# A 64-expert MoE on one core: the second expert product on column groups, and a sixteen-step pattern of heavy and light steps

## The chip, the core and the metric

The program runs on one core of a Trainium2 chip. The time is device microseconds of one execution; the kernel before took 1189.84 us (median of three runs, 1188.8 to 1190.72).

## What is computed

One layer of a hybrid decoder for 512 prompt tokens and 8 sample tokens (520 in all) of width 1024, in float32: a recurrent and convolutional mixer, cross-attention into 256 memory rows, and a mixture of experts, each followed by a residual and a layer norm. The change touches only the last:

```
scores = sigmoid(x @ w_router)                 # 64 experts, top 8 of each token, gates sum to 2.5
for each token t and each of its 8 experts e:
    h = silu(x[t] @ w1_e[e]) * (x[t] @ w3_e[e])        # 1024 -> 256, twice
    y[t] += gate[t, e] * (h @ w2_e[e])                 # 256 -> 1024
y += swiglu(x, w1_s, w3_s, w2_s)               # one shared expert
x = layer_norm(ALPHA * x + y)
```

520 tokens with 8 experts each make 4160 rows, 65 per expert on the mean. The weights of an expert are three matrices of 1 MB.

## The kernel before

Up to about 505 us the kernel does the mixer, the attention, the router and a sort of the experts by their number of rows. Then 64 steps follow, one per expert, and after them the sum over each token's eight rows and the last layer norm.

**Steps.** A step has one of three sizes. `LCAP` = 64 row slots is a light step, `MCAP` = 96 a heavy one, and `CAP` = 112 a big one, which is a heavy place among the first eight steps. The pattern has `NB` = 8 places with `LIGHT` = (2, 5, 7), so 24 experts get light steps and 40 heavy or big ones (35 heavy, 5 big). The sort gives the experts with the most rows to the heavy places. Should an expert have more rows than its step has slots, a second pass over all experts runs at the end (`n_max > CAP`; `bump` adds to the count what a step has less than 112).

**One step of TensorE** is written out as `step(e)`: `t_step(e-1)` transposes the hidden rows of the expert before; `c_step(e)` is the first product (`up_few`, `up_most` or `up`); `b_step(e+1)` transposes the gathered rows of the next expert; `y_step(e-1)` is the second product (`down_few` or `down`); `a_step(e+3)` finds the rows of the expert after (`find`, five small matmuls). `up_few` and `down_few` put two products of 64 columns side by side on the array's two column halves; `up_most` does so for 64 of its 96 slots, and puts the other 32 (`MORE`) four abreast on groups of 32 columns. The heavy second product is `down(..., MCAP)`: four matmuls of 96 columns by 512, on the whole array.

**The other engines.** ScalarE (ACT) copies the transposed rows (`xc`, `xc_part`), applies silu, copies the turned hidden rows (`hc_most`), and writes the left half of the result scaled by the gate (`yh`, L1650). VectorE (DVE) multiplies the hidden rows (`hd_most`, L2198), writes the right half of the result (`yh`, L2201), then turns found rows into indices (`indices`) and builds the one-hot rows of step e+5 (`oh`). GpSimd (POOL) waits for both halves of the result (`s_step`), scatters 64 rows and, of a heavy expert, the rest by `more_y` (L705), and only then issues the gather of expert e+3 (`g_step`, L692): 64 rows by `idx_x` and, for a heavy one, 32 more by `more_x`. TensorE's `b_step` waits for both.

**Weights.** SyncE (SP) has four weight slots. It issues the three loads of expert e+4 (L522 to L524) when the second product of expert e is done (`m_y`).

**The end.** When the scatter of expert 61 has landed, SP begins to load the 16 MB of `y_rows` back; TensorE sums them.

## Time and profile before

| | |
|---|---|
| median of 3 runs | 1189.84 us |
| profiled execution | 1188.33 us, of which the span from first to last instruction 1186.6 us |
| PE busy | 1129.1 us (95%) |
| DVE, ACT, POOL busy | 427.9, 256.9, 254.0 us |
| granted PE clock | 0.987 on the mean |
| HBM read and written | 300.15 and 29.36 MB |

Busy time says how long an engine had work, not what ended the program; for that the waits and the chain that ended last are read, and in the steps the order of work of TensorE beside the landing of what it needs. A PE record of a float32 matmul stands twice, since each is run as two passes.

### The profile page before, as it was taken

Reading aid. Unit: us, or ns where it says so; the run is one execution under the profiler, and the core shown is the slowest. Engines: PE = TensorE matmul, PEld = TensorE weight load, DVE = VectorE, ACT = ScalarE, POOL = GpSimd, SP = SyncE. Lnnn points to the kernel's source line nnn. Section 1 sums busy time; section 2 is a strip of 40 time slices with the busy share of each in tenths; the row PEclk is TensorE's granted clock in tenths of the full one; section 3 lists DMA queues with packets and bytes.
Section 4 is the critical chain, followed back from the end, with each engine's and each line's share of the span. In section 5 each row is a group of like instructions: output and inputs, shape, how many; then the busy total and the mean of one; then the engine's idle time right before and its main releaser. Section 6 shows DMA issues by size and latency. Waiting matters only on the chain.

```text
span 1186.6 us, 21423 instructions
## 1 busy us (share of the span) xinstructions
PE 1129.1 (95%) x8348; PEld 752.3 (63%) x8348; DVE 427.9 (36%) x1127; ACT 256.9 (22%) x533; POOL 254.0 (21%) x292
## 2 busy tenths in 40 slices
PE   7999996999999988989999999999999999999996
PEld 6888654877875767857765555555555565555521
DVE  0359998233039434661112222122222222221034
ACT  1101144013042124201122222222222222222210
POOL 3120050000000000032333333433323333333300
PEclk9999998999998999999999999999999999999999
DMA  9630304015045652185999999999999999999696
GB/s 331 250 142 1 152 21 177 1 75 227 1 143 176 250 214 108 73 286 197 365 408 392 396 383 394 402 399 388 383 386 402 393 384 384 381 401 387 260 369 279
DMA packets 67593, 319.16 MB, mean 269 GB/s; under 512 B 11591, under 2 KB 17951, under 8 KB 40909
## 3 DMA queue, kind: packets, MB, share of 16 engines
q1 hardware_dynamic: 51269, 278.60, 60.3%
q0 software_dynamic: 14848, 35.48, 7.9%
q10 hardware_dynamic: 1424, 4.35, 0.9%
q8 instruction: 37, 0.61, 0.2%
q14 instruction: 15, 0.12, 0.0%
HBM read 300.15 MB, written 29.36 MB: 278 GB/s over the span
## 4 chain that ended last, share of the span: by engine, by line
PE 74%; DVE 16%; DMA 4%; ACT 2%; SPq 2%; issue 1%; POOL 0%; DVEq 0%; POOLq 0%
PE psum L797 66%; PE psum L812 8%; DVE act_mem L1782 7%; DVE mk_mem L1944 2%; DMA arena<-y_rows 2%; DMA arena<-in_w_in_dram 1%; SPq L572 1%; DMA act_mem<-x_rows,more_x 1%; DVE act_mem L2000 0%; ACT act_mem L1565 0%; DVE act_mem L2151 0%; DVE act_mem L1879 0%; ACT act_mem L1574 0%; DVE act_mem L1796 0%; DVE act_mem L2163 0%
## 5 line engine op out<-in xcount | busy, mean ns | idle before, releaser
L797 PE MATMUL psum<-arena,act_mem 128*32 128x128 f32 (+6 forms) x4800 | 507.8, 361 | 0.9 <-ACT act_mem L1665 0.9
L797 PEld LDWEIGHTS psum<-arena,act_mem 128*32 128x32 f32 (+5 forms) x4800 | 259.7, 123 | 188.8 <-issue 107.9
L797 PE MATMUL psum<-act_mem,arena 128*128 128x260 f32 (+1 forms) x1728 | 355.1, 367 | 8.2 <-DMA arena<-in_w_in_dram 2.8
L797 PEld LDWEIGHTS psum<-act_mem,arena 128*128 128x128 f32 x1728 | 307.9, 194 | 52.8 <-DMA arena<-in_w_in_dram 3.0
L705 POOL DMA_INDIRECT y_rows<-act_mem,idx_y x39 | 45.9, 1177 | 239.3 <-DVE act_mem L2201 226.3
L812 PE MATMUL psum<-ident,act_mem 128*128 128x128 f32 (+6 forms) x484 | 80.0, 297 | 17.2 <-DVE act_mem L1883 6.8
L2201 DVE TENSOR_SCALAR act_mem<-psum,act_mem 96x512 f32<-96x512 f32 (+1 forms) x40 | 29.9, 747 | 159.7 <-PE psum L797 159.7
L1782 DVE SCALAR_TENSOR_TENSOR act_mem<-act_mem,wcb 128x511 f32<-128x511 f32 (+29 forms) x120 | 77.8, 729 | 0.0
L812 PEld LDWEIGHTS psum<-ident,act_mem 128*128 128x128 f32 (+6 forms) x484 | 58.5, 172 | 29.6 <-issue 13.7
L2198 DVE TENSOR_TENSOR act_mem<-act_mem,psum 128x192 f32<-128x192 f32 x35 | 12.4, 355 | 161.2 <-ACT act_mem L1636 161.2
L797 PEld LDWEIGHTS psum<-act_mem 128*96 128x96 bf16 (+7 forms) x419 | 31.3, 125 | 60.7 <-issue 59.7
L797 PE MATMUL psum<-act_mem 128*96 (+10 forms) x419 | 52.9, 264 | 0.8 <-DVE act_mem L2163 0.7
L1632 ACT ACTIVATE act_mem<-psum 128x768 f32<-128x768 f32 (+1 forms) x59 | 42.7, 724 | 45.6 <-PE psum L812 45.6
L1650 ACT ACTIVATE act_mem<-psum,act_mem 96x512 f32<-96x512 f32 (+1 forms) x40 | 27.4, 684 | 112.4 <-PE psum L797 112.4
L698 POOL DMA_INDIRECT y_rows<-act_mem,idx_y x23 | 25.3, 1102 | 117.0 <-DVE idx_x L2179 103.9
L1636 ACT ACTIVATE act_mem<-psum 128x192 f32<-128x192 f32 x35 | 11.6, 331 | 178.6 <-PE psum L797 178.6
L812 PE MATMUL psum<-ident,mk_mem 128*128 128x128 f32 (+5 forms) x316 | 43.6, 280 | 3.6 <-DVE mk_mem L1944 1.9
L812 PEld LDWEIGHTS psum<-ident,mk_mem 128*128 128x128 f32 (+5 forms) x316 | 36.9, 183 | 14.8 <-issue 12.4
L797 PE MATMUL psum<-arena,kv_mem 128*128 128x512 f32 x96 | 41.8, 593 | 1.2 <-ACT kv_mem L1454 1.2
L631 POOL MEMSET act_mem<- 128x512 f32 x1 | 0.5, 526 | 190.5 <-PE psum L812 190.5
L705 POOL DMA_INDIRECT y_rows<-act_mem,more_y x39 | 35.0, 897 | 11.9 <-issue 11.9
L692 POOL DMA_INDIRECT act_mem<-x_rows,idx_x x32 | 31.1, 973 | 15.0 <-issue 9.5
(282 smaller groups left out, 789.6 us busy)
## 6 DMA issues: line engine op xcount, KB each, us to landing
arena<-in_w_e_dram SPq DMA_DIRECT2D x192, 1024.0 KB, 9.8
arena<-y_rows SPq DMA_DIRECT2D x8, 2048.0 KB, 24.2
arena<-in_w_in_dram SPq DMA_DIRECT2D x16, 512.0 KB, 18.0
arena<-in_cache_mem_k_dram SPq DMA_DIRECT2D x8, 1024.0 KB, 8.6
arena<-in_cache_mem_v_dram SPq DMA_DIRECT2D x8, 1024.0 KB, 12.1
arena<-in_w_v_dram SPq DMA_DIRECT2D x1, 4096.0 KB, 24.7
arena<-in_w_k_dram SPq DMA_DIRECT2D x1, 4096.0 KB, 14.0
arena<-in_w_out_dram SPq DMA_DIRECT2D x1, 4096.0 KB, 14.0
```

The costliest lines, as they stand in the source:

```text
L572: sp.dma_start(y_in[t % 3][:, s], y.rearrange("(l s p) n -> s p l n", l=4, s=2)[s]).then_inc(s_yin[s][t % 3], 16)
L692: gp.indirect_dma_start(out=xg[b][at:at + cap, :], out_offset=None, in_=x2_rows[:, :], in_offset=bass.IndirectOffsetOnAxis(ap=idx[0:cap, n ...
L698: gp.indirect_dma_start(out=y_rows[:, :].rearrange("r (h n) -> (r h) n", h=2), out_offset=bass.IndirectOffsetOnAxis(ap=idx_y[:, n:n + 1], ...
L705: gp.indirect_dma_start(out=y_rows[:, :], out_offset=bass.IndirectOffsetOnAxis(ap=idx[0:cap, n:n + 1], axis=0), in_=src[at:at + cap, :], i ...
L797: return pe.matmul(out, lhsT, rhs, start=first, stop=last)
L812: return pe.transpose(out, in_, ident[0:n, 0:n])
L1632: return act.activation(xgT[:, b, :, 0:cap], psum[:, 1, :].rearrange("p (k s) -> p k s", k=KC)[:, :, ROWS_AT:ROWS_AT + cap], ACT.Copy)
L1650: return act.activation(out[0:cap, 0:512], psum[0:cap, 0, 0:512], ACT.Copy, scale=picked[0:cap, n, 1:2])
L1782: return dve.scalar_tensor_tensor(out, in0, w, in1, ALU.mult, ALU.add)
L1944: ins = dve.tensor_tensor_reduce(junk, kc[:, m, XD * h:XD * h + XD], q_all[:, b, XD * h:XD * h + XD], 1.0, 0.0, ALU.mult, ALU.add, ss[:, m ...
L2198: return dve.tensor_tensor(silu[:, b, 0:192], silu[:, b, 0:192], psum[:, 2, 512 * b + 192:512 * b + 384], ALU.mult)
L2201: return dve.tensor_scalar(out[0:cap, 512:1024], psum[0:cap, 0, 512:1024], picked[0:cap, n, 1:2], None, ALU.mult)
```

## The change

The heavy second product is split as the first one is: `down_most` computes the first 64 slots as two products of 64 columns by 512 side by side, and the other 32 as four of 32 columns by 256 abreast. Its result lies in PSUM in six pieces on other partitions than before, so ACT and DVE copy three pieces each (`yh_most`), and the gate is applied earlier, to the hidden rows (`hd_most`, with `gates` filled by `spread_gates`, six small copies). The pattern has 16 places of which seven are light, so 28 experts have light steps; 5 steps are big as before and 31 heavy. Waits on counters follow the new pattern in the parts not shown.

```diff
@@ -37,9 +37,10 @@
-NB = 8
-LIGHT = (2, 5, 7)
-HEAVY = (0, 1, 3, 4, 6)
+NB = 16
+BIGS = 8
+LIGHT = (2, 4, 6, 9, 11, 13, 15)
...
@@ -98,12 +99,12 @@
 
 
 def is_big(e):
-    return isinstance(e, int) and e < NB and e % NB in HEAVY
+    return isinstance(e, int) and e < BIGS and e % NB in HEAVY
 
 
 def turned(e):
 
-    return lights(e) if isinstance(e, int) and e < NB else e - (len(HEAVY) - 1)
+    return e + 1 - sum(1 for h in HEAVY if h < BIGS and (not isinstance(e, int) or h <= e))
 
 
 def heavies(k):
...
@@ -239,8 +240,9 @@
 
 
         table = act_mem[:, A4 + 320:A4 + 320 + 3 * TT * E].bitcast(BF16).rearrange("p (t e c) -> p t e c", t=TT, e=E)
-        picked = act_mem[:, A4 + 1280:A4 + 1280 + 2 * NB].rearrange("p (n c) -> p n c", c=2)
+        picked = act_mem[:, A4 + 1820:A4 + 1820 + 2 * NB].rearrange("p (n c) -> p n c", c=2)
         swT = act_mem[:, A4 + 1296:A4 + 1296 + T]
+        gates = act_mem[:, A4 + 1860:A4 + 1860 + 2 * NB].rearrange("p (n c) -> p n c", c=2)
         idx_y = sb("idx_y", [P, NB], U32)
         idx_x = sb("idx_x", [P, NB], U32)
         more_y = sb("more_y", [CAP - LCAP, NB], U32)
...
@@ -667,7 +669,7 @@
             for k in LIGHT:
                 gp.memset(bump[:, k:E:NB], float(CAP - LCAP)).then_inc(s_sortc, 1)
             for k in HEAVY:
-                gp.memset(bump[:, NB + k:E:NB], float(CAP - MCAP)).then_inc(s_sortc, 1)
+                gp.memset(bump[:, k if k >= BIGS else NB + k:E:NB], float(CAP - MCAP)).then_inc(s_sortc, 1)
             gp.memset(key_bias[:, 0:1], 65536.0).then_inc(s_sortc, 1)
             gp.memset(key_bias[:, 1:2], 49152.0).then_inc(s_sortc, 1)
             gp.memset(rank_at[0:E, E:2 * E], -1.0).then_inc(s_sortc, 1)
...
@@ -1271,6 +1273,19 @@
                                   wd[:, k, 512 * n:512 * n + 512], k == 0, k == 1)
                 return last
 
+            def down_most(b, part):
+
+                _, wd = ew(part)
+                for k in range(2):
+                    for h in range(2):
+                        mm(psum[LCAP * h:LCAP * h + LCAP, 0, 0:512], hidT[:, b, MCAP * k:MCAP * k + LCAP],
+                           wd[:, k, 512 * h:512 * h + 512], k == 0, k == 1)
+                for k in range(2):
+                    for q in range(4):
+                        last = mm(psum[MORE * q:MORE * q + MORE, 0, 512:768], hidT[:, b, MCAP * k + LCAP:MCAP * k + MCAP],
+                                  wd[:, k, 256 * q:256 * q + 256], k == 0, k == 1)
+                return last
+
             def a_step(e, n):
                 pe.wait_ge(m_oh, e + 1)
                 if at_least(e, 2):
...
@@ -1308,7 +1323,7 @@
                 if is_light(n):
                     down_few(n % 2, n % 4).then_inc(m_y, 1)
                 else:
-                    down(n % 2, n % 4, CAP if is_big(e) else MCAP).then_inc(m_y, 1)
+                    (down if is_big(e) else down_most)(n % 2, n % 4).then_inc(m_y, 1)
 
             wait_out(pe, "x24")
             a_step(0, 0)
...
@@ -1649,6 +1664,14 @@
             def yh(out, n, cap=CAP):
                 return act.activation(out[0:cap, 0:512], psum[0:cap, 0, 0:512], ACT.Copy, scale=picked[0:cap, n, 1:2])
 
+            def yh_most(out):
+
+                act.activation(out[0:LCAP, 0:512], psum[0:LCAP, 0, 0:512], ACT.Copy)
+                for q in range(2):
+                    last = act.activation(out[LCAP:MCAP, 256 * q:256 * q + 256],
+                                          psum[MORE * q:MORE * q + MORE, 0, 512:768], ACT.Copy)
+                return last
+
             def sl_few(b):
                 return act.activation(silu[:, b, 0:P], psum[:, 2, 512 * b:512 * b + P], ACT.Silu)
 
@@ -1682,8 +1705,10 @@
                     act.wait_ge(m_sm[n % 2], 16 * halves_out(i, k - 2, 2))
                 if is_light(n):
                     yh_few(n % 2, n).then_inc(m_ya, 1)
+                elif is_big(e):
+                    yh(ys[:, n % 2, :], n).then_inc(m_ya, 1)
                 else:
-                    yh(ys[:, n % 2, :], n, CAP if is_big(e) else MCAP).then_inc(m_ya, 1)
+                    yh_most(ys[:, n % 2, :]).then_inc(m_ya, 1)
 
             def step(e, k, i, sc):
                 if not is_big(e - 1):
...
@@ -2176,6 +2201,8 @@
                 if split:
                     dve.tensor_scalar(more_x[0:cap - LCAP, n:n + 1], more_y[0:cap - LCAP, n:n + 1], 3, None,
                                       ALU.logical_shift_right)
+                if spread:
+                    spread_gates(n)
                 return dve.tensor_scalar(idx_x[0:cap, n:n + 1], idx_y[0:cap, n:n + 1], 3, None, ALU.logical_shift_right)
 
             def indices_few(n, s, base_count):
...
@@ -2194,8 +2221,26 @@
             def hd(b):
                 return dve.tensor_tensor(hidT[:, b, :], silu[:, b, :], psum[:, 2, 512 * b + 2 * CAP:512 * b + 4 * CAP], ALU.mult)
 
-            def hd_most(b):
-                return dve.tensor_tensor(silu[:, b, 0:192], silu[:, b, 0:192], psum[:, 2, 512 * b + 192:512 * b + 384], ALU.mult)
+            def hd_most(b, n):
+
+                dve.scalar_tensor_tensor(silu[:, b, 0:P], silu[:, b, 0:P], gates[:, n, 0:1],
+                                         psum[:, 2, 512 * b + 192:512 * b + 320], ALU.mult, ALU.mult)
+                return dve.scalar_tensor_tensor(silu[:, b, P:192], silu[:, b, P:192], gates[:, n, 1:2],
+                                                psum[:, 2, 512 * b + 320:512 * b + 384], ALU.mult, ALU.mult)
+
+            def yh_most(out):
+
+                dve.tensor_copy(out[0:LCAP, 512:1024], psum[LCAP:2 * LCAP, 0, 0:512])
+                for q in range(2, 4):
+                    last = dve.tensor_copy(out[LCAP:MCAP, 256 * q:256 * q + 256], psum[MORE * q:MORE * q + MORE, 0, 512:768])
+                return last
+
+            def spread_gates(n):
+
+                for h in range(2):
+                    dve.tensor_copy(gates[LCAP * h:LCAP * h + LCAP, n, 0:1], picked[0:LCAP, n, 1:2])
+                for q in range(4):
+                    dve.tensor_copy(gates[MORE * q:MORE * q + MORE, n, 1:2], picked[LCAP:MCAP, n, 1:2])
 
             def yh(out, n, cap=CAP):
...
@@ -2219,13 +2264,17 @@
                 if is_light(n):
                     indices_few(n, m_iv, 2 * e).then_inc(m_idx, 1)
                 else:
-                    indices(n, m_iv, 2 * e, CAP if is_big(e) else MCAP).then_inc(m_idx, 1)
+                    indices(n, m_iv, 2 * e, CAP if is_big(e) else MCAP, spread=not is_big(e)).then_inc(m_idx, 1)
 
             def c_step(e, n):
                 dve.wait_ge(m_sl, e + 1)
                 if at_least(e, 2):
                     dve.wait_ge(m_y, e - 1)
-                (hd_few if is_light(n) else hd if is_big(e) else hd_most)(n % 2).then_inc(m_hd, 1)
+                if is_light(n) or is_big(e):
+                    (hd_few if is_light(n) else hd)(n % 2).then_inc(m_hd, 1)
+                else:
+                    dve.wait_ge(m_idx, e + 1)
+                    hd_most(n % 2, n).then_inc(m_hd, 1)
 
             def y_step(e, k, i, sc):
                 n = k % NB
@@ -2235,7 +2284,7 @@
                 if sc is not None:
                     dve.wait_ge(m_s[n % 2], sc)
                     dve.wait_ge(m_sm[n % 2], 16 * halves_out(i, k - 2, 2))
-                yh(ys[:, n % 2, :], n, CAP if is_big(e) else MCAP).then_inc(m_yv, 1)
+                (yh(ys[:, n % 2, :], n) if is_big(e) else yh_most(ys[:, n % 2, :])).then_inc(m_yv, 1)
 
             oh_step(0, 0)
```

## Rows read from the trace of the kernel before

**Rows 1.** The page's busy shares, and its slices of PE clock and DMA.

```profile
PE 1129.1 (95%) x8348; PEld 752.3 (63%) x8348; DVE 427.9 (36%) x1127; ACT 256.9 (22%) x533; POOL 254.0 (21%) x292
PEclk9999998999998999999999999999999999999999
DMA  9630304015045652185999999999999999999696
```

**Rows 2.** Waits by total between 560 and 1140 us: total us, times, longest us.

```profile
DVE act_mem L2198 <- ACT act_mem L1636: 161.2, 35, 5.7
PEld psum L812 <- DMA act_mem<-x_rows,more_x: 2.1, 2, 1.7
```

**Rows 3.** PE timeline: start us, us, line, out<-in, records, 805.8 to 823.6 us.

```profile
805.83 3.86 PE L797 MATMUL psum<-arena,act_mem 128*64 128x256 f32 x32
809.61 1.16 PE L812 MATMUL psum<-ident,mk_mem 128*128 128x128 f32 x8
810.61 3.60 PE L797 MATMUL psum<-arena,act_mem 128*96 128x512 f32 x8
814.04 0.35 PE L797 MATMUL psum<-act_mem 128*96 x5
814.49 5.83 PE L797 MATMUL psum<-arena,act_mem 128*64 128x256 f32 x96
820.25 1.16 PE L812 MATMUL psum<-ident,mk_mem 128*128 128x128 f32 x8
821.34 1.94 PE L797 MATMUL psum<-arena,act_mem 128*64 128x512 f32 x8
823.21 0.39 PE L797 MATMUL psum<-act_mem 128*96 x5
```

**Rows 4.** Busy by stretch: engines, then PE clock, DMA share, GB/s.

```profile
805.00:880.00 75.00, 75.00 (x758) 44.22 (x757) 16.05 (x55) 16.72 (x42) 26.24 (x26) 1.00 0.98 388
808.00:852.00 44.00, 44.00 (x445) 25.93 (x442) 8.15 (x29) 9.21 (x22) 15.46 (x16) 1.00 1.00 404
```

**Rows 5.** Chain that ended last, in order of time, its end.

```profile
1121.46 1.87 PE psum L797 x8
1149.97 26.55 DMA arena<-y_rows
```

**Rows 6.** POOL timeline: its first work after the sort constants.

```profile
502.20 0.14 POOL L680 IOTA small<- 128x5 f32 x1 [45.75 <-PE psum L812]
```

**Rows 7.** POOL timeline: the two gathers of step 24.

```profile
743.75 0.97 POOL L692 DMA_INDIRECT act_mem<-x_rows,idx_x  x1 [0.30 <-issue]
745.03 0.93 POOL L692 DMA_INDIRECT act_mem<-x_rows,more_x  x1 [0.30 <-issue]
```

**Rows 8.** PE timeline: end of step 20's product, transposes of step 24.

```profile
738.95 0.35 PE L797 MATMUL psum<-act_mem 128*96 x5
752.47 1.16 PE L812 MATMUL psum<-ident,act_mem 128*128 128x128 f32 x8
```

**Rows 9.** DVE groups by form: busy us, mean ns, idle before.

```profile
L2201 DVE TENSOR_SCALAR act_mem<-psum,act_mem 96x512 f32<-96x512 f32 x35 | 26.1, 747 | 140.9 <-PE psum L797 140.9
L2110 DVE COPY kv_mem<-psum 128x256 f32<-128x256 f32 x2 | 0.8, 422 | 2.1 <-PE psum L797 2.1
```

**Rows 10.** Gathers by more_x at 668.68, 745.03 and 1045.39 us: issue to landing.

```profile
DMA to landing us min/median/max: 8.7/8.7/8.7
DMA to landing us min/median/max: 7.0/7.0/7.0
DMA to landing us min/median/max: 5.9/5.9/5.9
```

**Rows 11.** SP's DMA issues: weights of step 11 and of the last step.

```profile
614.81 0.34 SPq L522 DMA_DIRECT2D arena<-in_w_e_dram  x1
1106.01 0.34 SPq L522 DMA_DIRECT2D arena<-in_w_e_dram  x1
```

**Rows 12.** The w2_e weight DMA, L524: issue to landing.

```profile
DMA to landing us min/median/max: 9.7/12.5/13.1
```

More of the change, by code:

```diff
@@ L39 @@
 ROUNDS = (T + CAP - LCAP + CAP - 1) // CAP
-NB = 8
-LIGHT = (2, 5, 7)
-HEAVY = (0, 1, 3, 4, 6)
+NB = 16
+BIGS = 8
+LIGHT = (2, 4, 6, 9, 11, 13, 15)
+HEAVY = (0, 1, 3, 5, 7, 8, 10, 12, 14)
 PAR_SPEC = [("b_in", 16), ("w_conv_a", 16), ("b_conv_a", 4), ("b_rg_a", 4), ("b_rg_x", 4), ("rg_lambda", 4),
@@ L1281, in b_step @@
                 n = k % NB
-                pe.wait_ge(m_g[n % 4], 16 * (2 * i + (k // 4 + 1)))
+                pe.wait_ge(m_g[n % 4], 16 * (NB // 4 * i + (k // 4 + 1)))
                 if not is_light(n):
@@ L1336, in step @@
                     t_step(e - 1, (k - 1) % NB)
-                c_step(e, k % NB, 48 * (2 * i + (k // 4 + 1)))
+                c_step(e, k % NB, 48 * (NB // 4 * i + (k // 4 + 1)))
                 if exists(e + 1):
@@ L2164, in oh, with indices @@
                                          numbers.unsqueeze(1).broadcast_to([P, TT, cap]), ALU.is_equal)
-            def indices(n, s, base_count, cap=CAP, split=True):
+            def indices(n, s, base_count, cap=CAP, split=True, spread=False):
                 at = 512 * (n % 2)
@@ L2276, in _ @@
             for k in range(1, NB + 1):
-                step(k, k, 0, None if k <= 2 else 16 * ((k - 1) // 2), None if k < 5 else 16 * ((k - 5) // 2 + 1))
+                step(k, k, 0, None if k <= 2 else 16 * ((k - 1) // 2), None if k < NB - 3 else 16 * ((k + 3 - NB) // 2 + 1))
             with dve.Fori(1, LAST) as i:
@@ L2280, in _ @@
                     step(NB * i + k, k, i, 16 * (NB // 2) * i + 16 * ((k - 1) // 2),
-                         16 * (NB // 2) * i + 16 * ((k - 5) // 2 + 1))
+                         16 * (NB // 2) * i + 16 * ((k + 3 - NB) // 2 + 1))
             for k in range(1, NB):
                 e = NB * LAST + k
-                step(e, k, LAST, 16 * ((e - 1) // 2), 16 * ((e - 5) // 2 + 1))
+                step(e, k, LAST, 16 * ((e - 1) // 2), 16 * ((e + 3 - NB) // 2 + 1))
             y_step(E - 1, NB - 1, LAST, 16 * ((E - 1) // 2))
```

## The prediction

> **What bounds the kernel now.** I read the page first [rows 1]: in the last two thirds of the span TensorE is busy nine tenths or more in every slice at full clock, and the DMA engines are equally full. So two resources are candidates. The waits [rows 2] choose between them: DVE waits 161 us before its 35 multiplications, while the only wait of TensorE for data in 580 us is 2.1 us for a gather. The order of time [rows 3] shows the same: a light first product (805.83 to the transposes at 809.6), a heavy second product from 810.61 to 814.04 (3.43 us), a heavy first product from 814.49 to 820.25 (5.76 us), a light second product from 821.34 to 823.21 (1.87 us), nothing idle between. TensorE sets the pace. But DMA stands just behind it [rows 4]: over 75 us, eight steps, it moves 388 GB/s at a share of 0.98; in the stretch without a drained queue it moves 404 GB/s at 1.00.
>
> **The end.** The chain [rows 5] goes from expert 61's second product (1121.46, 1.87 us) to the loads of `y_rows`, which run on DMA to 1176.5. That tail is the same work in both kernels. So what counts is how much earlier expert 61's second product ends. It ended at 1123.3.
>
> **Four experts from heavy to light.** 35 heavy steps become 31, 24 light ones 28. First product: 5.76 becomes 3.78 (805.83 to 809.61 [rows 3]), 1.98 less. Second: 3.43 becomes 1.87, 1.56 less, of which 0.09 is lost again, since the transposes ahead take 1.09 (820.25 to 821.34) where they take 1.00 ahead of a product on the whole array. 3.45 us each, 13.8 us for four.
>
> **The heavy second product on column groups.** It is not in this trace, but its halves are. Its first part is exactly the light product: 1.87 us. Its second has half of the columns' passes of that (16 records of 256 columns, four abreast, against 8 of 512, two abreast): 3.43 us for 8 records on the whole array is 0.43 each, a record of 256 is 0.21, 16 of them by four abreast 0.85. That four do run abreast is seen in the heavy first product: its 64 records of 128 columns (0.107 alone) add 5.76 - 3.78 = 1.98 us, where four abreast give 1.71 and one by one 6.8. The difference, 0.27, is the price of turning from two groups to four; I add it. So 1.87 + 0.85 + 0.27 + 0.09 = 3.08, against 3.43: 0.35 less. Bounds: 0.71 less if turning costs nothing (1.87 + 0.85), and 0.1 less if it costs twice what the first product pays. 30 heavy steps lie ahead of expert 61's end (all but place 62): 10.5 us, between 3 and 21.
>
> The Trainium skill ("TensorEngine Tiling (Array Packing)", Key Properties) says that changing the tiling mode drains the engine, which speaks against many short grouped parts. This case's rows agree with it by the 0.27 and the 0.09, and I take their size; no page gives one.
>
> TensorE alone thus saves 13.8 + 10.5 = 24.3 us.
>
> **What hides, and behind what.** The sort's constants on POOL grow from 16 small operations to 32, about 0.1 us each; POOL has then nothing to do for 45.75 us, up to 502.2 [rows 6], and the first product that uses them comes late in that time. Without that cover they would cost 2 us. `spread_gates` puts six copies of about 0.14 us ahead of `idx_x` on DVE, queued behind `yh_most`. The indices are then ready some 1.5 us later than now, 4 us after the product; the gather that needs them starts 4.8 us after it (738.95 to 743.75 [rows 7, 8]) and later still in the new kernel. Behind them on DVE stands the one-hot of step e+5 and the next multiplication, for which DVE now waits 4 to 5 us in each step [rows 2]: covered. `hd_most` in two pieces costs 0.2 us of the same cover. The first eight steps have the same five big and three light ones, in another order: nothing.
>
> **The copies are not hidden everywhere.** DVE's copy of 512 columns takes 0.75 us now, and a copy of 256 takes 0.42 [rows 9]. Afterwards DVE does one of 512 and two of 256, so the last would end 0.84 us later one by one; I estimate 0.67, since the long one no longer multiplies and short ones overlap a little. ACT does as much, with pieces no longer than DVE's. POOL waits for both halves before it scatters, and queued behind the scatters stands the gather. So each gather that follows a heavy expert starts 0.67 us later.
>
> Who waits for it? Let me take the narrowest place, where heavy, light, heavy, light, heavy follow each other. Here [rows 7, 8]: product of expert 20 ends at 738.95, and behind its two scatters the gathers start, by `idx_x` at 743.75, by `more_x` at 745.03; expert 24's transposes begin at 752.47. The gather has 7.4 us before it costs anything. In this pattern that narrow place comes once in eight steps. Its landings were 8.7 us at step 16, 7.0 at 24, and 5.9 at 56, the last of the six [rows 10], as the experts have fewer rows: only the first cost a wait, 8.7 - 7.4 = 1.3 us. In the new pattern the same place comes five times in sixteen steps (the expert four places on is heavy too, with one heavy between two lights): 17 times before expert 61's end, at steps 12, 14, 16, 21, 23, 28 and so on. And the room is 7.4 - 0.67 = 6.75 us. With the landings as they are now: 1.95 us at steps 12, 14, 16; about 0.75 at 21 and 23; next to nothing after, where 7.0 falls to 5.9. Sum 7.4 us, of which 1.3 is paid already: 6 us more. Bounds: no more than 0 if they land in 6 us everywhere, and 17 x 1.25 - 1.3 = 20 us if all land in 8 us.
>
> **Sum.** 24.3 - 6 = 18 us less for the end of expert 61, and so for the end. The profiled execution (1188.33, span 1186.6 and 1.7 around it) becomes 1170.3. It ran 1.5 us under the median, so in the median's terms 1171.8. I forecast 1172.
>
> **Rivals.**
> *DMA becomes the bound.* Eight steps move 388 x 75 = 29.1 MB, 3.64 MB a step, at 404 GB/s 9.0 us a step; in the fuller first periods up to 9.1. The 52 steps between the two issues in [rows 11] took 491.2 us, 9.45 each, and TensorE's saving brings that to 9.0. Saturated from the issue at 614.81, whose last load lands at 628.3 (about 1 us for the two loads issued ahead of it, 12.5 to land [rows 12]), expert 62's weights land 51 x 9.0 to 9.1 later, at 1087 to 1092, and expert 61's product, behind 62's first product and a transpose, ends 9 us after, at 1096 to 1101. That is a saving of 22 to 27 us: a floor that catches TensorE's best case (a heavy product 0.71 us shorter) but lies beyond my forecast. For it: the share of 1.00. Against it: the four slots give two steps, 18 us, from issue to use, and 13.5 are used. Result about 1167. The Trainium skill ("HBM Reference", the table's note on a core alone) puts a core that streams alone at about 425 GB/s; by it the floor would lie at 8.6 us a step and would never be met. The long undrained stretch here shows 404, and I go by that.
>
> *Turning is dearer.* If a heavy second product gains only 0.1 us, 7 us of the saving go: 1179.
>
> *The gather turn sets the pace, on the other side.* From product to scatter to gather to transposes is a ring through DVE, POOL and DMA that TensorE can't shorten. It takes 24.3 / 17 = 1.4 us per narrow place, over and above the 1.3 us now paid once, to eat the whole saving: that is when the gathers there land in 8.2 us or later on the mean. Many gathers elsewhere do land late, and a fuller DMA queue or two engines that now read one PSUM bank at the same time would push that way. At 8.7 us, as at step 16, each place costs 1.95: 33 - 1.3 - 24.3 = 7.5 us slower, 1197. Against it: after the first of the six present narrow places, the landings went from 7.0 to 5.9 us.
>
> *The second pass runs.* If one of the 28 light experts had over 64 rows, all experts would be passed again, milliseconds. The reference's own router on its seeded inputs gives 32 experts over 64 rows and none over 96; 36 places are heavy. I give it one in a hundred.
>
> **How the numbers follow.** Forecast (1169 to 1177) 0.45; DMA floor or a cheaper product, 1164 to 1169, 0.20; turning dearer, or gathers landing late, 1177 to 1187, 0.24; the ring eats it all, 1187 to 1192, 0.06, or turns it slower, 0.04; the second pass 0.01. The range 1165 to 1184 leaves out 0.05 below and 0.15 above. A change under 0.2% (2.4 us) can't be told from none here. Faster by more: 0.88; within: 0.05; slower: 0.07.
>
> **What the profile after would show.** Heavy second product 3.0 to 3.1 us with 24 records; light to heavy turn unchanged; DVE's last piece 0.67 us later and POOL's scatter with it; waits of TensorE's transposes for `more_x` of 1 to 2 us at steps 12 to 16, small from 28 on; no wait for weights; expert 61's product at about 1105, the tail after it unchanged. I am wrong if heavy products stay at 3.4 us, if waits for gathers go on to the last steps, or if DMA never drains and weights land last.

## The result, and the profile after

The changed kernel takes 1182.54 us, the median of six runs (1180.74 to 1185.17), beside 1190.07 for the kernel before on the same chip (1187.94 to 1190.72): a ratio of 0.9942 [0.9927, 0.9956], 7.5 us faster. The forecast was 1172, 18 us faster. The profiled execution took 1182.73 us, its span 1180.9. Lines have moved by two: L799 is the product that was L797, L814 the transpose, L694 the gather, L524 the first load of an expert's weights.

The page of the kernel after: busy time of TensorE, its clock and the DMA share in 40 slices, and the queue that loads instructions (packets, MB, share).

```profile
PE 1106.9 (94%) x8584; PEld 733.6 (62%) x8584; DVE 484.7 (41%) x1394; ACT 278.2 (24%) x587; POOL 245.6 (21%) x300
PEclk9999998999998989999999999999899999999998
DMA  9630304016034752183999999999899999999696
q8 instruction: 72, 1.18, 0.4%
```

TensorE's busy time fell by 22.2 us [rows 1], but the time by 7.5, so TensorE now stands still, or runs slowly, for long enough to lose two thirds of it. Two things are new in the slices: in the middle of the stretch that was 9 throughout, at slice 29, both the clock and the DMA share show an 8. (The clock's 8 in the last slice belongs to the tail, below.) And the queue of instructions has 72 packets; before the change it had 37:

```profile
q8 instruction: 37, 0.61, 0.2%
```

The heavy second product, from the timeline of TensorE after the change (start us, us, records):

```profile
768.56 1.16 PE L814 MATMUL psum<-ident,mk_mem 128*128 128x128 f32 x8
769.65 2.94 PE L799 MATMUL psum<-arena,act_mem 128*64 128x512 f32 x24
772.52 0.39 PE L799 MATMUL psum<-act_mem 128*96 x5
786.82 1.15 PE L814 MATMUL psum<-ident,act_mem 128*128 128x128 f32 x8 [0.75 <-DMA act_mem<-x_rows,more_x]
```

Start to start it takes 2.87 us (769.65 to 772.52), where it took 3.43 [rows 3]; the transposes ahead cost 0.09 more, as before a grouped product. So 0.47 is gained, not 0.35. The last row is another thing: transposes that waited for a gather. The waits between 560 and 1140 us (in total, times, longest) show how often:

```profile
PE psum L814 <- issue: 8.9, 8, 3.5
PEld psum L814 <- DMA act_mem<-x_rows,more_x: 7.5, 6, 1.9
PEld psum L814 <- DMA mk_mem<-x_rows,idx_x: 4.4, 3, 1.7
PEld psum L814 <- DMA act_mem<-x_rows,idx_x: 2.7, 3, 1.1
```

Before the change there were two waits of this kind, 2.1 us [rows 2]. (A weight load waits while the product ahead still runs, so these sums are more than TensorE lost; the intervals below tell that.) The first row is new too. "issue" means that the profile shows nothing that was waited for. Six of its eight, 5.2 us together, stand ahead of transposes of gathered rows, at places where the step is long as well; I count them as waits for gathers. One more is under 0.3 us. The eighth has nothing to do with data. It is 3.5 us long, and here it is on the timeline, where the loop over sixteen steps jumps back, after step 32:

```profile
834.65 1.94 PE L799 MATMUL psum<-arena,act_mem 128*64 128x512 f32 x8
836.52 0.39 PE L799 MATMUL psum<-act_mem 128*96 x5
840.44 0.68 PE L814 MATMUL psum<-ident,act_mem 128*128 128x128 f32 x2 [3.54 <-issue]
841.05 8.24 PE L799 MATMUL psum<-arena,act_mem 128*64 128x256 f32 x96
```

A heavy first product that takes 5.83 us elsewhere [rows 3] takes 8.24 here. The windows of 2 us around it (busy time and records of each engine, then TensorE's granted clock, DMA share, GB/s):

```profile
838.00:840.00 2.00, 0.00 (x0) 0.00 (x0) 1.15 (x5) 0.00 (x0) 1.52 (x2) 0.85 1.01 387
842.00:844.00 2.00, 2.00 (x12) 1.12 (x10) 0.00 (x0) 0.00 (x0) 0.00 (x0) 0.50 0.99 406
848.00:850.00 2.00, 2.00 (x53) 1.79 (x44) 0.30 (x2) 0.33 (x1) 0.00 (x0) 1.00 0.26 100
```

While TensorE stood still the granted clock began to fall, and for some 6 us after it it was 0.50, the lower level of 1.2 GHz. From one issue of weights to the next this step takes 16.7 us, the same kind of step elsewhere 10.3: 6.4 us for one jump back.

SP issues an expert's weights when the product of the expert four places earlier has ended, so its issues are a clock of the steps. The two that answer to [rows 11]:

```profile
617.74 0.34 SPq L524 DMA_DIRECT2D arena<-in_w_e_dram  x1
1098.01 0.34 SPq L524 DMA_DIRECT2D arena<-in_w_e_dram  x1
```

The 52 steps between take 480.3 us, 10.9 less than before. The first stands 2.9 us later than before: 1.4 of that is there already at the first product (548.3 against 546.9; with the same code ahead of it this point lies anywhere from 543.6 to 549.1 in the runs below), and 1.5 are two waits for gathers within the first eight steps. The chain that ended last:

```profile
1114.34 1.87 PE psum L799 x8
...
1142.97 26.81 DMA arena<-y_rows
```

Expert 61's product ends at 1116.2 (1123.3 before [rows 5]), 7.1 us earlier. One more wait for a gather, 1.16 us ahead of the transposes of expert 62, lies between the end of the 52 steps and that product.

The tail does the same work as before but took 64.7 us here and 63.3 before, so the spans differ by 5.7 us and not by 7.1. Most of that is TensorE's last product, before the change and after it:

```profile
1176.56 1.92 PE L797 MATMUL psum<-arena,sum_rows 128*32 128x512 f32 x16 [2.88 <-DMA arena<-y_rows]
1169.83 3.05 PE L799 MATMUL psum<-arena,sum_rows 128*32 128x512 f32 x16 [2.79 <-DMA arena<-y_rows]
```

Over the last 13 to 14 us the granted clock was 0.82 before and 0.59 after. From SP's last issue to the end the traces of this document take anything from 80.6 to 83.0 us, written-out and looped kernels alike, so I take this as a difference between executions.

### The profile page after: what moved, and what is told of

It is laid out like the page before. It is cut to its first block, busy times and chain, and to the rows that moved or that the text cites. A ratio compares the mean times of both kernels' runs of the same rounds, so it can differ in the third digit from the quotient of the medians.

```text
span 1180.9 us, 21870 instructions
## 1 busy us (share of the span) xinstructions
PE 1106.9 (94%) x8584; PEld 733.6 (62%) x8584; DVE 484.7 (41%) x1394; ACT 278.2 (24%) x587; POOL 245.6 (21%) x300
## 3 DMA queue, kind: packets, MB, share of 16 engines
q8 instruction: 72, 1.18, 0.4%
## 4 chain that ended last, share of the span: by engine, by line
PE 62%; DVE 18%; DMA 11%; issue 3%; ACT 2%; SPq 2%; POOL 1%; DVEq 0%; POOLq 0%
PE psum L799 56%; DVE act_mem L1807 7%; PE psum L814 6%; DMA act_mem<-x_rows,more_x 4%; DVE mk_mem L1969 2%; DMA arena<-y_rows 2%; DMA mk_mem<-x_rows,idx_x 2%; DMA act_mem<-x_rows,idx_x 1%; DMA arena<-in_w_in_dram 1%; SPq L574 1%; POOL y_rows L707 1%; DVE act_mem L2235 1%; POOL act_mem L694 0%; DVE act_mem L2025 0%; ACT act_mem L1580 0%
## 5 line engine op out<-in xcount | busy, mean ns | idle before, releaser
L799 PE MATMUL psum<-arena,act_mem 128*32 128x128 f32 (+5 forms) x5040 | 476.8, 371 | 1.6 <-ACT act_mem L1688 1.6
L799 PE MATMUL psum<-act_mem,arena 128*128 128x260 f32 (+1 forms) x1728 | 356.6, 369 | 8.5 <-DMA arena<-in_w_in_dram 3.4
L799 PEld LDWEIGHTS psum<-arena,act_mem 128*32 128x32 f32 (+3 forms) x5040 | 241.0, 122 | 187.5 <-issue 98.7
L799 PEld LDWEIGHTS psum<-act_mem,arena 128*128 128x128 f32 x1728 | 309.3, 194 | 53.3 <-DMA arena<-in_w_in_dram 3.0
L814 PE MATMUL psum<-ident,act_mem 128*128 128x128 f32 (+6 forms) x480 | 78.4, 294 | 29.1 <-DVE act_mem L1908 6.8
L707 POOL DMA_INDIRECT y_rows<-act_mem,idx_y x35 | 39.8, 1136 | 251.6 <-DVE act_mem L2235 204.1
L814 PEld LDWEIGHTS psum<-ident,act_mem 128*128 128x128 f32 (+6 forms) x480 | 57.3, 171 | 42.9 <-issue 18.6
L2233 DVE COPY act_mem<-psum 64x512 f32<-64x512 f32 x31 | 21.5, 693 | 117.8 <-PE psum L799 117.8
L799 PEld LDWEIGHTS psum<-act_mem 128*96 128x96 bf16 (+7 forms) x419 | 28.1, 124 | 56.5 <-issue 55.5
L799 PE MATMUL psum<-act_mem 128*96 (+10 forms) x419 | 53.1, 264 | 0.8 <-DVE act_mem L2188 0.7
L2226 DVE SCALAR_TENSOR_TENSOR act_mem<-act_mem,psum 128x128 f32<-128x128 f32 x31 | 10.8, 348 | 104.4 <-ACT act_mem L1651 104.4
L814 PE MATMUL psum<-ident,mk_mem 128*128 128x128 f32 (+5 forms) x316 | 43.4, 280 | 8.3 <-issue 2.5
L700 POOL DMA_INDIRECT y_rows<-act_mem,idx_y x27 | 27.3, 1013 | 105.6 <-ACT act_mem L1679 63.3
L814 PEld LDWEIGHTS psum<-ident,mk_mem 128*128 128x128 f32 (+5 forms) x316 | 36.9, 184 | 19.8 <-issue 12.9
L1651 ACT ACTIVATE act_mem<-psum 128x192 f32<-128x192 f32 x31 | 10.3, 332 | 145.6 <-PE psum L799 145.6
L799 PE MATMUL psum<-arena,kv_mem 128*128 128x512 f32 x96 | 41.8, 593 | 1.2 <-ACT kv_mem L1469 1.2
L2219 DVE TENSOR_TENSOR act_mem<-act_mem,psum 128x128 f32<-128x128 f32 x28 | 8.1, 288 | 71.6 <-ACT act_mem L1676 71.6
L1443 ACT ACTIVATE act_mem<-psum,par 128x520 f32<-128x520 f32 x24 | 16.1, 696 | 81.8 <-PE psum L799 81.7
## 6 DMA issues: line engine op xcount, KB each, us to landing
arena<-in_cache_mem_v_dram SPq DMA_DIRECT2D x8, 1024.0 KB, 12.1
```

What stands on the lines that cost most here:

```text
L700: gp.indirect_dma_start(out=y_rows[:, :].rearrange("r (h n) -> (r h) n", h=2), out_offset=bass.IndirectOffsetOnAxis(ap=idx_y[:, n:n + 1], ...
L707: gp.indirect_dma_start(out=y_rows[:, :], out_offset=bass.IndirectOffsetOnAxis(ap=idx[0:cap, n:n + 1], axis=0), in_=src[at:at + cap, :], i ...
L799: return pe.matmul(out, lhsT, rhs, start=first, stop=last)
L814: return pe.transpose(out, in_, ident[0:n, 0:n])
L1443: act.activation(out, two(bank(name)), func, **kw).then_inc(s_emA, 1)
L2226: dve.scalar_tensor_tensor(silu[:, b, 0:P], silu[:, b, 0:P], gates[:, n, 0:1], psum[:, 2, 512 * b + 192:512 * b + 320], ALU.mult, ALU.mult)
```

## The experiments

The first group takes the change apart.

**The split product alone**, in the old pattern of eight steps.

```diff
-NB = 16
+NB = 8
-LIGHT = (2, 4, 6, 9, 11, 13, 15)
-HEAVY = (0, 1, 3, 5, 7, 8, 10, 12, 14)
+LIGHT = (2, 5, 7)
+HEAVY = (0, 1, 3, 4, 6)
```

> Only the second product on column groups, in the old pattern of eight steps (24 experts on 64 slots). My theory: TensorE gains 0.47 us in each of 34 heavy steps, 16 us; the loop of eight steps shows no stall at its return; the one narrow place in eight steps (heavy, light, heavy, light, heavy) now waits about 1 us for its gather, some 6 us more than before. Sum: 10 us faster than the kernel before. Rival (the split product itself costs more than it gives, through the copies): no faster than before. Rival (the stall near step 32 belongs to the split product and not to the long loop): a pause of 3 us or more of TensorE at a loop's return is in this trace too.

Measured: 1207.39 us (1203.67 to 1210.17), 1.0141 [1.0118, 1.0164], 17 us *slower* than before. Every jump back now has a pause, and there are five. One of them, from TensorE's timeline:

```profile
769.35 0.39 PE L799 MATMUL psum<-act_mem 128*96 x5
774.02 0.47 PE L814 MATMUL psum<-ident,act_mem 128*128 128x128 f32 x2 [4.29 <-issue]
774.43 7.37 PE L799 MATMUL psum<-arena,act_mem 128*64 128x256 f32 x96
```

The intervals at steps 16, 24, 32, 40 and 48 are 16.0, 16.4, 17.2, 15.9 and 16.0 us where 10.3 is normal: 29.8 us lost in all. Without them the kernel would stand 12 us below the one before, which is what the product should give. Its queue of instructions moves 83 packets, 1.36 MB, the kernel before 37. The gain that was expected is there, buried under these pauses.

**The pattern alone**, with the old second product.

```diff
-                    (down if is_big(e) else down_most)(n % 2, n % 4).then_inc(m_y, 1)
+                    down(n % 2, n % 4, CAP if is_big(e) else MCAP).then_inc(m_y, 1)
```

(with the copies and gates as they were)

> Only the pattern of sixteen steps with 28 light ones; the heavy second product, its two copies and the gate as before the change. My theory: four lighter steps give 13.8 us, the stall at the loop's return takes 6 us, and 17 narrow places with the gather at its old start wait about 0.4 us each where one wait of 1.3 was before, 6 us. Sum: 0 to 3 us faster than before. Rival (waits for gathers come only from the later copies): 6 to 9 us faster, with hardly a wait for gathers. Rival (the stall belongs to the new product): no stall, 8 us faster or more.

Measured: 1190.2 us (1187.24 to 1193.99), 1.0011 [0.9997, 1.0026]: no gain at all. The step at the jump takes 18.4 us for 10.9, 7.5 lost, and about 7 go to waits for gathers.

**The changed kernel with TensorE's loop written out**, so that it has no jump. The instructions and their order are the same.

```diff
-            with pe.Fori(1, LAST) as i:
+            for i in range(1, LAST):
```

> The changed kernel with TensorE's loop over two times sixteen steps written out, so that TensorE never jumps back; the other engines keep their loops. My theory: the pause of 3.5 us after step 31's product and the half clock after it (2.5 us) are the price of the jump back over a long loop body, and go: 6 us faster than the changed kernel, 13 us faster than before. Rival (the pause has another cause at that time, such as an instruction transfer or another engine's jump): it stays, and the time is that of the changed kernel.

Measured: 1174.35 us (1172.33 to 1182.95), 0.9885 [0.9856, 0.9914], 8 us less than the changed kernel. Step 32 is back at 10.3, but step 33 takes 12.1 instead of 8.2, so the two steps together give back 2.5 us and not 8. The rest of the 8.9 us between the two profiled executions lies elsewhere: waits for gathers are 3.2 us shorter in the 52 steps, 1.3 us lie ahead of the first product and 2.0 in the tail. That these come from writing out the loop is not shown. First TensorE's timeline there, then DVE's:

```profile
846.52 0.44 PE L814 MATMUL psum<-ident,act_mem 128*128 128x128 f32 x2 [2.11 <-DVE act_mem L2228]
846.89 5.44 PE L799 MATMUL psum<-arena,act_mem 128*64 128x256 f32 x32
```

```profile
841.15 0.35 DVE L2226 SCALAR_TENSOR_TENSOR act_mem<-act_mem,psum 128x128 f32<-128x128 f32 x1 [4.66 <-ACT act_mem L1651]
846.19 0.28 DVE L2228 SCALAR_TENSOR_TENSOR act_mem<-act_mem,psum 128x64 f32<-128x64 f32 x1 [4.69 <-issue]
```

DVE's own loop jumps back at 835.4 in this trace; its next instruction starts at 840.9, and then 4.69 us of "issue" stand between the two halves of one multiplication. Both times a packet of the second queue of instructions, q14, had landed 1.5 us before DVE went on. Under TensorE's pause it did not matter; now it holds TensorE for 2.1 us and the clock falls again (5.44 us for a light first product of 3.8).

**The split alone again, with TensorE's loop written out.**

> The split second product in the old pattern of eight steps (17 us slower than before, with a pause at five of TensorE's jumps back), with TensorE's loop written out. My theory: the split product is good by itself and loses only by making the loop body too long; without the jumps 30 us come back, 10 us or more faster than the kernel before. Rival (the pauses come from the split product at these steps, whatever the loop): pauses of 4 us every eight steps stay, and the time stays near 1207 us.

Measured: 1179.55 us (1177.0 to 1182.21), 0.9907 [0.9892, 0.9921]. The same work with and without five jumps: 28 us apart, which agrees with the 29.8 read from the intervals. Freed of them, the split product is worth 10.4 us here.

The second group asks whether it is the length of the loop's body. Before the change the body, by the calls in the code, has 437 matmuls on TensorE, and the steps at its jumps take no longer than their like. (The trace records 1618 instructions of TensorE in one pass: a float32 product stands twice, every multiplication has a weight load, and 104 more wait, count and branch.) **The kernel before with the five small matmuls that find an expert's tokens done twice** in every step has 477; what it computes is the same.

```diff
+                find(n, e, P if is_light(n) else CAP if is_big(e) else MCAP)
                 find(n, e, P if is_light(n) else CAP if is_big(e) else MCAP).then_inc(m_ip, 1)
```

> The kernel before, in which the five small matmuls that find the rows run twice in each step, with the same result; this adds 40 matmuls to TensorE's loop body of eight steps, as many as the split product adds. My theory: the length of the body alone makes the jump back dear; pauses appear at the jumps (steps 16, 24, 32, 40, 48), 6 to 7 us each with the slower clock behind them, beside 0.1 to 0.2 us of work in each step: 35 to 45 us slower than before. Rival (the pause is made by the split product or the sixteen-step pattern): no pauses, 6 to 12 us slower from the added work.

> The same as the run with the row-finding matmuls twice, with TensorE's loop written out. My theory: no jump, no pause; only the added work stays, 6 to 12 us slower than before. Rival: as slow as with the loop.

> The kernel before with TensorE's loop of eight steps written out, nothing else. My theory: its trace shows no pause at a jump, so there is nothing to gain; within 0.2% of before. Rival (every jump back costs something, even in a short body, or written-out code is better in itself): 2 us or more faster.

Measured: with the loop 1261.5 us, 1.0596 [1.0577, 1.0616] (one of its six executions took 3853.7 us; the ratio leaves it out), written out 1199.44 (1197.18 to 1202.13), 1.0079 [1.0062, 1.0096]. Forty small matmuls in 437, worth 9.5 us as work, cost 62 more as length, where 35 to 45 in all were expected; the pauses with the slow stretch behind each take about 12 us. And the kernel before, written out, takes 1189.16 (1186.21 to 1195.36), 1.0008 [0.9994, 1.0022]: it had nothing to win there.

**The same in the light steps only**, 15 matmuls more, a body of 452.

```diff
+                if is_light(n):
+                    find(n, e, P)
                 find(n, e, P if is_light(n) else CAP if is_big(e) else MCAP).then_inc(m_ip, 1)
```

> The kernel before with the row-finding matmuls run twice in the light steps only, same result: 15 matmuls more in TensorE's loop body of eight steps (437 become 452), where 40 more gave pauses of 10 us at every jump. My theory: the pause sets in at some length between 437 and 477; if under 452 there are pauses at steps 16, 24, 32, 40 and 48 again and 25 us or more are lost, if over 452 it is 2 to 4 us slower from the added work alone. Rival (the pause grows in proportion to the length): a small pause of some 4 us at each jump, 20 us slower.

Measured: 1228.91 us (1224.99 to 1230.9), 1.033 [1.0311, 1.035], 40 us slower for 15 small matmuls. The pause is there in full at every jump, on TensorE's timeline:

```profile
779.10 0.68 PE L812 MATMUL psum<-ident,act_mem 128*128 128x128 f32 x2 [5.25 <-issue]
779.72 8.45 PE L797 MATMUL psum<-arena,act_mem 128*64 128x256 f32 x96
```

So it begins between these two bodies, of 437 and 452 matmuls, 1618 and 1648 recorded instructions. The added matmuls also lengthen the steps ahead of the loop, so the length of the body and its place in the code changed together; no run separates the two. The size does not grow with the body: with the slow stretch about 7 us at 452, 5.5 to 6.9 at 477 (the split alone), 12 at 477 (twice), 7.5 at 841 (the pattern alone), 6.4 at 913 (the changed kernel).

The queue of instructions shows what goes with the pause. Between 690 and 1065 us, over five jumps back, the kernel before moves nothing on it. The split alone moves the first row there, and the same written out the second:

```profile
q8 instruction: 43, 0.70, 0.7%
q8 instruction: 34, 0.56, 0.5%
```

And in each of the 18 pauses at a jump of TensorE that these traces hold (the changed kernel 1, the split alone 5, the pattern alone 1, find twice 5, in the light steps only 5, gather first 1) a packet starts while TensorE stands still. This is the window 836.91 to 840.44 of the changed kernel, the 3.5 us shown above, and then the window 778.77 to 788.78 of the kernel that finds twice, one of its pauses of 10 us:

```profile
q8 instruction: 1, 0.02, 1.7%
q8 instruction: 2, 0.03, 1.2%
```

TensorE goes on 1.2 to 2.0 us after the last such packet has landed, all 18 times. The seven pauses of 3.5 to 4.3 us have one packet in them, the eleven of 4.8 to 10.0 us have two. Why two packets lie 1 us apart in some kernels and 6 us in another these runs do not show.

The third group is about the gathers. **The changed kernel with POOL issuing the gather of expert e+3 ahead of the scatters of expert e-1.** The gather writes a buffer that has long been read; only the order in POOL's queue made it wait for the copies.

```diff
-                    s_step(NB * i + (k - 1), k - 1, i)
                     g_step(NB * i + (k + 3), (k + 3) % NB)
+                    s_step(NB * i + (k - 1), k - 1, i)
```

> The changed kernel, but GpSimd issues the gather of step e+3 ahead of the scatter of step e-1 and no longer behind it, so that the gather waits for its indices alone and not for the copies of the result. My theory: gathers start about 2 us earlier after a heavy step, the 11 us of waits for gathers go, the stall at the loop's return stays: 10 us faster than the changed kernel, 17 us faster than before. Rival (gathers land late because the DMA engines are full, and an earlier start only lengthens their stay): landing times grow by what the start gains, and the time stays. Rival (DMA throughput is already the bound): waits move from gathers to weights, and less than 4 us come back.

Measured: 1169.71 us (1167.1 to 1171.06), 0.9826 [0.9804, 0.9847], 12.8 us less than the changed kernel. Its waits, 560 to 1140 us:

```profile
PE psum L814 <- issue: 4.3, 1, 4.3
PEld psum L814 <- DMA act_mem<-x_rows,more_x: 2.5, 6, 0.4
PEld psum L814 <- DMA act_mem<-x_rows,idx_x: 1.0, 1, 1.0
```

The waits for gathers are down from 14.6 to 3.5 us, mostly under the product that still runs, and the pause at the jump stays.

**The kernel before with the same turn of the queue.**

> The kernel before with the gather of step e+3 issued ahead of the scatter of step e-1. My theory: the room for the gather was only just enough before, and one wait of 1.3 us is all there is to win; 0 to 2 us faster. Rival (an earlier gather is worth as much to any pattern): 8 us or more faster, as in the changed kernel.

Measured: 1188.85 us (1185.04 to 1192.29), 1.0005 [0.9995, 1.0015]. The old pattern left the gathers their time; there is nothing to win.

**Both cures in the changed kernel**: gather first, and the loops of TensorE, ACT, DVE and POOL written out.

> The changed kernel with the gather of step e+3 issued ahead of the scatter of step e-1, and the loops over the steps written out on all four compute engines. My theory: on top of gather-first (20 us faster than before) the stall of 6.6 us at step 32 goes, and with it the pause that a written-out TensorE alone moved to step 33, where it waited for VectorE's jump back: 26 to 27 us faster than before. Rival (DMA becomes the bound at 9.0 to 9.1 us a step): TensorE begins to wait for weights and it stays within 3 us of gather-first. Rival (written-out code costs elsewhere, by its own transfers): pauses at other places, no better than gather-first.

Measured: 1164.4 us (1162.08 to 1166.93), 0.979 [0.9774, 0.9806], the fastest of all: 25.5 us less than the 1189.9 beside it, 18 less than the changed kernel. SP's issues, and two of five windows of 75 us, which are much alike:

```profile
614.88 0.34 SPq L524 DMA_DIRECT2D arena<-in_w_e_dram  x1
1079.59 0.34 SPq L524 DMA_DIRECT2D arena<-in_w_e_dram  x1
```

```profile
725.00:800.00 75.00, 73.96 (x835) 43.68 (x830) 23.28 (x90) 20.67 (x52) 26.39 (x28) 1.00 1.01 411
875.00:950.00 75.00, 74.73 (x830) 43.14 (x830) 25.94 (x99) 20.36 (x51) 23.61 (x25) 1.00 1.01 414
```

52 steps in 464.7 us are 8.94 a step, at 411 to 414 GB/s, and no wait for weights among the waits. One pause is new, 1.04 us of "issue" at 747.9 in the midst of written-out code, and it ends as a packet of the queue of instructions lands. The 8.94 is under the 9.0 to 9.1 that my rival gave as DMA's floor.

**The same without the split product**, to price it free of waits and jumps.

> The pattern of sixteen steps alone (old second product and copies), gather first, all four loops written out; against the same with the split product (25.5 us faster than before) it gives the worth of the split product when neither waits for gathers nor jumps stand in its way. My theory: 30 times 0.47 us, so this is 14 us slower than that one and 11 to 13 us faster than before. Rival (the later copies still cost the split product something, or DMA holds it back): the two differ by less than 10 us.

Measured: 1172.76 us (1172.07 to 1176.52), 0.9863 [0.9849, 0.9877]; 8.4 us above the last one by the medians, 9.4 by what each gains over the kernel before beside it. In its trace:

```profile
617.01 0.34 SPq L524 DMA_DIRECT2D arena<-in_w_e_dram  x1
1092.28 0.34 SPq L524 DMA_DIRECT2D arena<-in_w_e_dram  x1
```

475.3 us for the 52 steps, 10.6 more than with the split product, and 11.7 more if the pause at 747.9, which this kernel does not have, is left out. So the split is worth 8 to 12 us, and not the 14 that were expected.

## Why the prediction was right and where it failed

**TensorE's work: right.** The two terms were 13.8 and 10.5 us, together 24.3. In the traces with few waits and no jumps the pattern gives 491.2 - 475.3 = 15.9 us, less the 1.3 that the kernel before paid for its one gather, 14.6; the split gives 10.6, or 11.7 without the pause at 747.9, and 0.5 more for expert 60, whose product ends behind the 52 steps. Together 26.8. Within the split two errors partly cancel: the product gains 0.47 us and not 0.35, so turning from two groups to four costs less than the 0.27 that I took from the first product (1.87 + 0.85 = 2.72 against 2.87, so 0.15); but light steps' intervals behind heavy ones are about 0.1 us longer than before (9.15 against 9.06). The rival of dearer turning is out.

**The step that failed first: the sum had no term for the loop.** The part that costs the change names products, copies, constants and gates, and takes the steps around them as they were. But the change doubles the body of the loop that the steps stand in, from 437 matmuls to 913. That took away four of the five jumps back and made the one that is left cost 6.4 us: 3.5 us of pause and the rest at half clock. The old kernel's jumps cost nothing, so no row of its trace could have warned me; the split product alone, with 40 matmuls more in the old body, loses 29.8 us to it. Written out, the loop gives 28 us back there. In the changed kernel it gives 6.4 back at the step of the jump, of which DVE's pause behind it takes 3.9 again. The Trainium skill ("Runtime: NRT & Kernel Launch", Instruction fetch mechanics) says that a taken branch whose target is outside the instructions at hand forces a fetch by DMA, and calls it a stall. The traces agree: the kernels with the pause move 68 to 83 packets on the queue of instructions instead of 37, some 16 KB each (1.18 MB in 72), the kernel before moves none while it jumps back five times, and all 18 pauses end 1.2 to 2.0 us after a packet has landed. A high count alone is not the pause: kernels written out move 65 to 72 packets, most with no pause of this kind and one with one of 1.04 us. So the pause is shown to be the jump's, and that it waits for the instructions rests on the order of time in the traces; no run changes the fetch by itself. The Trainium skill gives no price for it.

**The second step: the waits for gathers were sized at 7.4 us and are 13.0.** The places were right. Against the kernel with both cures, step for step, the waits fall on experts 12, 14, 21, 28, 30, 32, 37, 44, 53, 55, 60 and 62, with next to nothing at 16, 23, 39, 46 and 48. The sizes were not: experts 12 to 23 cost 3.8 us where I had 7.4, and those from 28 on cost 7.7 where I had next to nothing; two more, 1.5 us, fell on experts 5 and 7 in the first eight steps, which I had called unchanged. (TensorE's idle time ahead of the transposes of gathered rows, read from its timeline, adds up to 13.3.) I had read three landings of the old trace, 8.7, 7.0 and 5.9 [rows 10], as a fall, and gave it a reason, fewer rows for an expert. All gathers between 620 and 1100 us from issue to landing, first the 83 before the change and then the 81 after it:

```profile
DMA to landing us min/median/max: 5.9/7.7/9.4
```

```profile
DMA to landing us min/median/max: 6.5/7.9/9.3
```

The 5.9 was the smallest of 83, and the spread is the same after. The trend was none. In the changed kernel the narrow places have landings like any others; two of POOL's rows, behind the product that ended at 772.5:

```profile
777.76 0.97 POOL L694 DMA_INDIRECT act_mem<-x_rows,idx_x  x1 [0.30 <-issue]
779.04 0.93 POOL L694 DMA_INDIRECT act_mem<-x_rows,more_x  x1 [0.30 <-issue]
```

The second starts 6.5 us after the product's end, where it was 6.1 (738.95 to 745.03 [rows 7, 8]): the delay by the copies, 0.67 in the forecast, is 0.4 here. It lands after 7.7 us, at 786.7, and the transposes start at 786.82. With a median landing of 7.9 and a room that I had put at 6.75, the forecast's own rule would have given about 1.15 at each of 17 places, nearly 20 us; the true room is wider by the smaller delay, and what was measured lies between that and the 7.4. Moving the gather ahead of the scatters takes most of the waits away and 12.8 us with them, by the medians.

**The balance.** -26.8 for TensorE, +6.4 for the jump, +13.0 - 1.3 for gathers: -8.7. The end of expert 61's product moved by -7.1; 1.4 of start-up that differs between executions of the same code makes up nearly all of the rest. The forecast's 24.3 - 6.1 = 18.2 differs from the 8.7 by 6.4 of a term that was not there and 5.6 of one that was too small (11.7 for 6.1), less 2.5 that TensorE's work gave above its forecast. The time lies inside the range of 1165 to 1184, but that range was made wide for dearer turning and late gathers; about half of the miss came from a jump that it knew nothing of.

**The rivals.** *DMA as the bound* was wrong in its floor: I had taken the 404 GB/s of an undrained stretch [rows 4] for the most that the core can move, and 8.94 us a step at 411 to 414 stands under the 9.0 that followed from it. The Trainium skill's 425 GB/s ("HBM Reference", Specifications (TRN2)) is not reached either, but the floor that I set against it was the worse one. *The ring of the gathers* was the right mechanism with the right places; it eats 11.7 of the gain, not all. *The second pass* did not run.

**What I had hidden and was hidden:** the constants, the gates and the two-part multiplication. None of them appears among the waits of TensorE.

## What to carry to other kernels

Before a change that lengthens or doubles the body of a hardware loop, count what it will issue on each engine, and afterwards compare the step at the jump back with its like elsewhere: nine per cent more matmuls in the body (437 to 477) turned a 10 us gain into a 17 us loss, and writing the loop out gave it back. A few landings picked at the places of interest are draws from a spread; take the median and the ends of all of them before a wait is priced. And in a queue that both fetches and stores, look whether the fetch must stand behind the store: here the order alone was worth 12.8 us once steps were short, and nothing while they were long.

## What was not expected of the hardware

- A jump back of TensorE's loop costs nothing with 437 matmuls in the body and 5.5 to 12 us with 452 to 913, the half clock behind it included; it begins between these kernels of 437 and 452, and the size does not follow the length. A packet of the queue of instructions starts in every such pause, and TensorE goes on 1.2 to 2.0 us after the last has landed. DVE has pauses of this kind too, one of 4.69 us.
- A pause of 3.5 to 10 us on TensorE costs more than itself: behind the 3.54 us the granted clock was 0.50 for some 6 us, and a product of 5.8 us took 8.2.
- DMA moved 411 to 414 GB/s over windows of 75 us, with a share of 1.01 to 1.02, in a mix of weight loads, gathers and scatters that had shown 388 over 75 us, and 404 over the 44 us without a drained queue, before.
- A heavy second product in 24 grouped records takes 2.87 us against 3.43 on the whole array, 0.15 above the 2.72 worked out from its parts.
